# Nine expert-weight buffers and an fp32r scatter in a mixture-of-experts stage

## The reference

```python
hn2 = rms_norm(x, g_norm2) * (1.0 + scale2) + shift2
g_prob = softmax(hn2 @ w_rg + b_rg)                 # 4 groups, the best one is taken
e_top, e_loc = top_k(e_logits_of_that_group, 2)     # 2 of its 8 experts
e_w = softmax(e_top) * g_w
ffn[token] = sum over its 2 experts e of e_w * ((silu(h @ w_gate[e]) * (h @ w_up[e])) @ w_down[e])
x = x + gate2 * ffn
return rms_norm(x, g_final)
```

## Time and profile before

| | us |
|---|---|
| median of 3 runs | 1523.45 (1521.31 to 1524.22) |
| the profiled execution | 1520.18 |
| its span, first to last instruction | 1518.3 |
| PE busy | 1396.9 (92%) |
| DVE busy | 697.5 (46%) |
| ACT busy | 577.2 (38%) |
| POOL busy | 69.7 (5%) |
| DMA, mean over the span | 245 GB/s |

### The profile page before, as it was taken

The page is one execution under the profiler, slowest core; times in us unless marked ns, Lnnn a source line. Parts: engine busy times, 40 slices in busy tenths (PEclk is TensorE's granted clock), DMA queues, the critical chain, the costliest instruction groups (busy, mean ns, idle before and its releaser), DMA issues.

```text
span 1518.3 us, 20243 instructions
## 1 busy us (share of the span) xinstructions
PE 1396.9 (92%) x7966; PEld 1004.9 (66%) x7966; DVE 697.5 (46%) x1208; ACT 577.2 (38%) x869; POOL 69.7 (5%) x75
## 2 busy tenths in 40 slices
PE   6999889999899967899997998879999999999995
PEld 6988578888679845899985985554444444444442
DVE  4744556666455445677755655552112112112113
ACT  4343645555544394565554543321111111111111
POOL 1000000101000033100000002000000000000000
PEclk9999999999999977999998996789999999999998
DMA  8547237899443601265644453055999999999991
GB/s 312 203 169 274 84 111 240 299 315 355 174 167 141 247 1 56 78 199 179 222 169 150 158 175 111 0 221 224 415 429 428 429 429 429 429 428 428 428 429 77
DMA packets 105634, 372.48 MB, mean 245 GB/s; under 512 B 4189, under 2 KB 51581, under 8 KB 93169
## 3 DMA queue, kind: packets, MB, share of 16 engines
q1 hardware_dynamic: 97680, 344.07, 58.6%
q0 software_dynamic: 7904, 27.76, 5.3%
HBM read 370.75 MB, written 1.05 MB: 245 GB/s over the span
## 4 chain that ended last, share of the span: by engine, by line
PE 68%; DMA 17%; DVE 7%; ACT 3%; issue 2%; POOL 1%; SPq 0%; DVEq 0%; ACTq 0%; POOLq 0%
DMA ring<-in_w_expert_up_dram 16%; PE ps L522 14%; PE ps L1211 10%; PE ps L488 8%; PE ps L489 7%; PE ps L490 7%; PE ps L501 3%; PE ps L503 3%; PE ps L502 3%; PE ps L1232 2%; DVE w_low L425 2%; PE ps L1186 2%; PE ps L899 2%; PE ps L1194 1%; DMA ring<-in_ret_w_in_dram 1%
## 5 line engine op out<-in xcount | busy, mean ns | idle before, releaser
L425 DVE TENSOR_TENSOR w_low<-ring,w_high 128x1024 fp32r<-128x1024 f32 x260 | 307.8, 1225 | 244.1 <-ACT w_high L417 236.5
L417 ACT ACTIVATE w_high<-ring 128x1024 fp32r<-128x1024 f32 x264 | 264.8, 1052 | 232.8 <-PE ps L522 109.4
L488 PE MATMUL ps<-h_high,w_high 128*128 128x256 f32 x1088 | 312.7, 287 | 4.5 <-DVE w_low L425 2.6
L489 PE MATMUL ps<-h_low,w_high 128*128 128x256 f32 x1088 | 308.9, 284 | 0.0
L490 PE MATMUL ps<-h_high,w_low 128*128 128x256 f32 x1088 | 308.7, 284 | 0.0
L1211 PE MATMUL ps<-ring,arena 128*64 128x512 f32 x1024 | 224.9, 593 | 8.1 <-DMA ring<-in_w_expert_up_dram 6.3
L488 PEld LDWEIGHTS ps<-h_high,w_high 128*128 128x128 f32 x1088 | 209.8, 193 | 24.3 <-issue 18.9
L489 PEld LDWEIGHTS ps<-h_low,w_high 128*128 128x128 f32 x1088 | 209.9, 193 | 0.0
L490 PEld LDWEIGHTS ps<-h_high,w_low 128*128 128x128 f32 x1088 | 209.7, 193 | 0.0
L1211 PEld LDWEIGHTS ps<-ring,arena 128*64 128x64 f32 x1024 | 77.4, 137 | 152.4 <-issue 152.4
L2036 DVE TENSOR_TENSOR arena<-arena,ps 128x512 f32<-128x512 f32 x16 | 16.7, 1046 | 219.3 <-PE ps L1211 219.3
(11 more groups left out here) (327 smaller groups left out, 1506.0 us busy)
## 6 DMA issues: line engine op xcount, KB each, us to landing
ring<-in_w_expert_down_dram SPq DMA_DIRECT2D x32, 2048.0 KB, 12.3
ring<-in_w_expert_gate_dram SPq DMA_DIRECT2D x32, 2048.0 KB, 14.9
ring<-in_w_expert_up_dram SPq DMA_DIRECT2D x32, 2048.0 KB, 17.2
ring<-in_ffn_w_up_dram SPq DMA_DIRECT2D x44, 1024.0 KB, 7.7
ring<-in_ret_w_in_dram SPq DMA_DIRECT2D x11, 2048.0 KB, 8.2
ring<-in_ffn_w_down_dram SPq DMA_DIRECT2D x10, 2048.0 KB, 9.5
ring<-in_w_in_dram SPq DMA_DIRECT2D x7, 2048.0 KB, 8.1
gates<-in_w_ada_dram POOLq DMA_DIRECT2D x12, 1024.0 KB, 5.7
```

Source lines behind the costliest of these rows:

```text
L417: nc.scalar.activation(hi, raw, ACT.Copy).then_inc(hi_done, 1)
L425: last = eng.tensor_tensor(lo, raw, hi.bitcast(F32), ALU.subtract)
L488: nc.tensor.matmul(o, hi, hTh[:, k, :], start=(k == 0), stop=False)
L489: nc.tensor.matmul(o, hi, hTl[:, k, :], start=False, stop=False)
```

## The change

Buffers. `const` keeps only the tables that are used late; decay, cosine and sine go to the end of the arena (a second DMA at the start). The arena grows by them, and three new slots, 6 to 8, lie in its last 12288 columns. Their order of use is `HOMES`; tile N (two gates, two ups, two downs per pair) goes to `HOMES[N % 9]` when tile N - 9 has been used. Slots 6 to 8 wait for `l_t`. The last two down tiles come in halves. The router's four small loads move on POOL from the start of the mixer to behind `l_t`, since their place in the arena is used until then.

Arithmetic. PSUM banks 0 to 3 start with x (products with the identity). The weight of a token goes into the hidden layer (`wslot`, the maximum over a row of the turned selection), the selection for the scatter becomes 0/1, the down result is multiplied by gate2 and split in `y_hi` and `y_lo` (fp32r), and the scatter is eight fp32r products. The last norm reads PSUM, tile by tile.

Order. The loop runs over three pairs per trip. The scatter of pair j comes after the gate products of pair j + 1. The gather's first half comes before the turn of the hidden layer, its second behind it. After the last pair no further gather is done. The flag is loaded before the last pair's end instead of behind it.

```diff
+        HOMES = (2, 6, 7, 8, 0, 1, 3, 4, 5)
+        NS = len(HOMES)
+        TILES = 3 * NE
...
+        def landed(N):
+
+            s = HOMES[N % NS]
+            return ring_in[s], last_fill[s] + 16 * (N // NS + 1)
+
+        def used(N):
+
+            p, c = N // 6, N % 6
+            return (m_gu, 2 * p + 1 + c // 2, 2) if c < 4 else (m_dn, p + 1, 1)
...
+            def expert_load(N, i=None):
+                s, value, step = used(N - NS)
+                sp.wait_ge(s, value if i is None else i * (3 * step) + value)
+                dst, src, done = expert_tile(N, i)
+                sp.dma_start(dst[:, :, :], src).then_inc(done, 16)
...
+            for N in range(NS):
+                home = HOMES[N]
+                if home < 3:
+                    sp.wait_ge(*freed[holder[home]])
+                elif home < 6:
+                    sp.wait_ge(wide_mm, n_halves)
+                else:
+                    sp.wait_ge(l_t, 2)
+                dst, src, done = expert_tile(N)
+                sp.dma_start(dst[:, :, :], src).then_inc(done, 16)
...
+            pool.wait_ge(l_t, 2)
             pool.dma_start(wr[:, :, 0:NG], A["w_router_group_2"][0].rearrange("(p k) n -> p k n", p=P)).then_inc(r_in, 16)
...
-            clear_sums(2)
+            for t in range(NT):
+                for half in range(2):
+                    nc.tensor.matmul(ps[:, 2 * t + half, :], ident, x[:, t, half * C:(half + 1) * C], start=True,
+                                     stop=False, skip_group_check=True)
```

On TensorE the scatter and the loop:

```diff
+            def scatter(j, i=None):
+
+                pe.wait_ge(m_swt, at(j + 1, i, 3))
+                pe.wait_ge(m_ya, at(2 * j + 2, i, 6))
+                pe.wait_ge(m_yv, at(2 * j + 2, i, 6))
+                for t in range(NT):
+                    for y in (y_hi, y_lo):
+                        for half in range(2):
+                            last = nc.tensor.matmul(ps[:, 2 * t + half, :], selT[:, t * P:(t + 1) * P],
+                                                    y[:, half * C:(half + 1) * C], start=False, stop=False,
+                                                    skip_group_check=True)
+                    if t == 0 and i is None:
+                        last.then_inc(m_fin, 1)
+                last.then_inc(m_fin if i is None else m_sct, 1)
...
-                gather((PAIRS + 2) * r + 1, None)
-                with pe.Fori(0, PAIRS) as i:
...
-                    scatter(False)
-                    pe.wait_ge(m_h, i + (PAIRS * r + 1))
...
-                    gather(i + ((PAIRS + 2) * r + 2), i + (PAIRS * r + 1))
...
-                scatter(True)
+                first = PAIRS * r
+                for half in range(2):
+                    gather(first, half)
+                gate_or_up(first, 0)
+                turn_select(first)
+                with pe.Fori(0, PAIRS // 3) as i:
+                    for j in range(first, first + 3):
+                        gate_or_up(j, 1, i)
+                        gather(j + 1, 0, i)
+                        turn_hidden(j, i)
+                        gather(j + 1, 1, i)
+                        pe.wait_ge(m_hc, at(j + 1, i, 3))
+                        homes = [enter_tile(6 * j + 4 + e, i) for e in range(2)]
+                        down(homes, range(KE)).then_inc(m_dn, 1)
+                        gate_or_up(j + 1, 0, i)
+                        turn_select(j + 1, i)
+                        scatter(j, i)
+                j = first + PAIRS - 1
+                gate_or_up(j, 1)
+                turn_hidden(j)
+                pe.wait_ge(m_hc, j + 1)
+                for e in range(2):
+                    pe.wait_ge(half_in[e], 16 * (r + 1))
+                homes = [HOMES[(6 * j + 4 + e) % NS] for e in range(2)]
+                down(homes, (0, 1))
+                for e in range(2):
+                    enter_tile(6 * j + 4 + e)
+                down(homes, (2, 3)).then_inc(m_dn, 1)
+                scatter(j)
```

On ScalarE and VectorE:

```diff
+            def silu(j, i=None):
+                act.wait_ge(m_gu, at(2 * j + 1, i, 6))
+                if j % PAIRS:
+                    act.wait_ge(m_sct, at((PAIRS - 1) * (j // PAIRS) + j % PAIRS, i, 3))
+                nc.scalar.activation(hs, ps[:, 4, :], ACT.Silu).then_inc(m_si, 1)
...
+            nc.scalar.activation(credit[:, 7:8], const[:, 0:1], ACT.Sqrt)
+            expert_end(0)
...
-            norm_act(act, 7)
+                    expert_end(r)
+                act.wait_ge(m_fin, NT * PASSES)
+            for t in range(NT):
+                act.wait_ge(m_fin, t + 1)
+                nc.scalar.activation(xn[:, t, :].rearrange("p (h n) -> p h n", h=2), ps[:, 2 * t:2 * t + 2, :], ACT.Square,
+                                     accum_out=stat[:, 20 + t:21 + t]).then_inc(f_ss, 1)
+                act.wait_ge(f_ms, t + 1)
+                nc.scalar.activation(stat[:, 24 + t:25 + t], stat[:, 22 + t:23 + t], ACT.Sqrt).then_inc(f_sd, 1)
...
+            def turned(j, i=None):
+
+                dve.wait_ge(m_tr, at(j + 1, i, 3))
+                if j % PAIRS:
+                    dve.wait_ge(m_sct, at((PAIRS - 1) * (j // PAIRS) + j % PAIRS, i, 3))
+                nc.vector.tensor_reduce(wslot, ps[:, 6, 0:T], AX, ALU.max)
+                nc.vector.tensor_scalar(selT[:, :], ps[:, 6, 0:T], 0.0, None, ALU.is_gt).then_inc(m_swt, 1)
...
+            def gated(j, i=None):
+                dve.wait_ge(m_dn, at(j + 1, i, 3))
+                for half in range(2):
+                    cols = slice(half * C, (half + 1) * C)
+                    nc.vector.tensor_tensor(ye[:, cols], ps[:, 6 + half, :], gates[:, 1, cols], ALU.mult).then_inc(m_y, 1)
+                for half in range(2):
+                    cols = slice(half * C, (half + 1) * C)
+                    dve.wait_ge(m_ya, at(2 * j + 1 + half, i, 6))
+                    nc.vector.tensor_tensor(y_lo[:, cols], ye[:, cols], y_hi[:, cols].bitcast(F32), ALU.subtract)\
+                        .then_inc(m_yv, 1)
```

More of the change, by code:

```diff
@@ L526, in project, with gated_residual @@
                 last.then_inc(wide_mm, 1)
[L528 removed]
+        def gated_residual(link, g, bank, tmp, tiles):
             for t in tiles:
@@ L1176, in _ @@
             nc.tensor.matmul(ps[:, 5, 128:128 + NE], ones, asg[:, 1, :], start=False, stop=True).then_inc(t_lg, 1)
-            def gather(value, hgt):
-                pe.wait_ge(m_s, value)
-                for half in (1, 0):
-                    if half == 0 and hgt is not None:
-                        pe.wait_ge(m_hc, hgt)
-                    for k in range(4 * half, 4 * half + 4):
-                        for t in range(NT):
-                            last = nc.tensor.matmul(ps[:, 4 + half, (k % 4) * P:(k % 4 + 1) * P],
-                                                    xn[:, t, k * P:(k + 1) * P], sel[:, t, :],
-                                                    start=(t == 0), stop=(t == NT - 1))
-                    last.then_inc(m_ga, 1)
@@ new lines, in at, with gather @@
+            def at(value, i, step):
+                return value if i is None else i * step + value
+            def gather(j, half, i=None):
+                if half == 0:
+                    pe.wait_ge(m_s, at((PAIRS + 1) * (j // PAIRS) + j % PAIRS + 1, i, 3))
+                if j:
+                    pe.wait_ge(m_h if half else m_si, at(j, i, 3))
+                for k in range(4 * half, 4 * half + 4):
+                    for t in range(NT):
+                        last = nc.tensor.matmul(ps[:, 4 + half, (k % 4) * P:(k % 4 + 1) * P],
+                                                xn[:, t, k * P:(k + 1) * P], sel[:, t, :],
+                                                start=(t == 0), stop=(t == NT - 1))
+                last.then_inc(m_ga, 1)
@@ new lines, in enter_tile, with gate_or_up @@
+            def enter_tile(N, i=None):
+                s, value = landed(N)
+                pe.wait_ge(s, at(value, i, 32))
+                return HOMES[N % NS]
+            def gate_or_up(j, g, i=None):
+                if g == 0:
+                    pe.wait_ge(m_xa, at(j + 1, i, 3))
+                    pe.wait_ge(m_xv, at(j + 1, i, 3))
+                homes = [enter_tile(6 * j + 2 * g + e, i) for e in range(2)]
+                for k in range(KD):
+                    for e in range(2):
+                        last = nc.tensor.matmul(ps[e * R:(e + 1) * R, 4 + g, :], xg[:, k, e * R:(e + 1) * R],
+                                                wide[homes[e]][:, k, :], start=(k == 0), stop=(k == KD - 1))
+                last.then_inc(m_gu, 1)
@@ new lines, in down @@
+            def down(homes, ks):
+                for half in range(2):
+                    for k in ks:
+                        for e in range(2):
+                            last = nc.tensor.matmul(ps[e * R:(e + 1) * R, 6 + half, :], hgT[:, k, e * R:(e + 1) * R],
+                                                    tall[homes[e]][:, k, half * C:(half + 1) * C],
```

(35 more changed lines are left out.)

367 lines of the change are left out of this document (176 added, 191 removed).

## The result

The changed kernel takes 1495.5 us (median of 4 runs, 1494.17 to 1496.84); the kernel before, on the same chip, 1522.38 us. The ratio is 0.9823, with a 95% interval of 0.9806 to 0.984: faster by 1.8%. The forecast was 1495.4 us. Two later groups of runs on other occasions gave 1496.0 and 1496.54, beside 1523.17 and 1523.7 for the kernel before. The profiled run took 1494.17 us, 26.0 less than the profiled run of before; the working had foreseen 28.0. So the forecast's agreement with the median hides terms that were off by up to 1.8 us, and the rest of this document looks for them.

What follows compares the result with a forecast made beforehand. The stream of expert tiles was taken to bound the stage, narrowly ahead of TensorE. Gains of 17.0, 5.3 and 5.8 us, less 0.1 for the start, made 28.0 off 1523.45: 1495.4 us, range 1489 to 1506.

Steps and rivals of the forecast that it cites:

- Nine slots: Expert stage: three more tiles fetched before the first pair, so 87 instead of 90 remain after it; 14.7 us saved.
- The second hole: Stream loss at 1060 to 1080 us (387 of 429 GB/s), because down tiles' buffers come free late; 2.0 us saved.
- The price of a tile: Expert stream from 1042.0 us: one tile takes 4.894 us, from 90 tiles moved until 1484.5.
- TensorE per pair: Expert stage: a pair takes TensorE 27.4 us instead of 28.56, with scatter 1.97 and stall 0.35, against 29.4 of stream.
- Upper bound ... 28.9, which still hides: If fp32r scatter costs as much as fp32, a pair takes TensorE 28.9 us, still hidden under 29.4 of stream.
- TensorE binds: Rival: unseen hand-overs add 3 us a pair, so a pair takes 30.3 us and the kernel 1507; chance 0.10.
- The last pair: From the last up tile's landing to the last down's end: 16.8 us instead of 22.1, gain 5.3 us.
- The rival of the falling clock: Expert stage: at 1.2 GHz TensorE needs 54 us a pair; three pairs of sixteen give 1570 us; chance 0.04.
- The tail: From the last down's end to the kernel's end: 13.4 us instead of 19.2, gain 5.8 us.
- The rival of late tables: Router's four table DMAs, moved beside the tile stream, delay the router from 1010.38: +8.6 us, 1504; chance 0.09.
- The start: Kernel start: constants come in two DMAs instead of one, costing zero to 0.4 us; 0.1 taken off the gain.
- The signs: Wrong if data ends after 1470, router starts later, a mid-stage pair takes other than 29.4 us, or clock leaves 1.00.

Runs made afterwards that it cites:

- the upper group's with the later wait: Changed kernel with VectorE's wait for the constants put behind the third weight tile's split; its slower runs, 1503.31, 1503.85 and 1507.28 us, at first; 6 of 11 near 1504.

## Why the prediction held, and where its steps did not

*Nine slots, 14.7 us.* Right: 14.8 by six against nine slots. *The second hole, 2.0 us.* Right: 2.0, and by the order: it stayed closed with six slots, and with the fp32 scatter. *The price of a tile.* (1468.7 - 1042.4) / 87 = 4.90 us against 4.894, with 1042.4 from the 223 GB/s of 1040 to 1045.

*TensorE per pair.* 27.3 to 27.5 us against 27.4: right, but two terms were off against each other. The scatter takes 1.85 us, not 1.97, and the stall for the hidden copy was almost nothing, 0.03 to 0.05 in the chain, not 0.35, while the other steps came out that much longer.

*"Upper bound ... 28.9, which still hides", and "nothing of this reaches the end time".* This step is wrong, though it did no harm at 27.4. I compared periods, 28.9 with 29.4, and should have compared ends. TensorE's sum is 1041.0 (first up) + 15 x 27.4 = 1452.0; the stream's is 1460.8. The margin is 8.8 us in fifteen pairs, 0.6 us a pair. The fp32 scatter of 29.0 us a pair ended at 1478.7. So the slots and the cheap scatter are worth their 15 to 16 us only together, and the rival "TensorE binds", which I let begin with 3 us more a pair, begins with 0.6. For the same reason TensorE does not wait "for DMA before both gate and up" in the whole stage but only from 1333 us on.

*The last pair, 5.3 us.* The path was right (16.8 us in the run with six slots), its size here was not: 18.5 us, since the down product ran partly at the lower clock and took 8.81 instead of 7.04. The text had kept the clock high for the whole of the stage because it was 1.00 in the earlier trace rows; between the pairs it was, with idle times of at most 1.2 us (1.5 in the run with half the scatter). Behind the last up, TensorE is idle for 1.24 us, does four short turns and is idle for 0.69 us, and the clock is at 0.50 from about 1471 to 1474 us. With TensorE kept busy the down took 7.1 us in three of three profiles. The gaps alone do not say where the fall comes: of the ten profiles with the same two gaps, seven have it in the down, and three (six slots, the fp32 scatter, the upper group's with the later wait) kept 1.00 through the down and fell in the last scatter, as two of the three filled ones did. Of all the profiles here only that with 10 and 5 filling matmuls shows neither. So that the gaps bring the fall is likely and not shown, and so is what decides its place. The rival of the falling clock was thus right in its kind and wrong in its place and size: not 54 us a pair in mid-stage but 1 to 2 us, once. The Trainium skill, "TensorE: Matmul & The Clock Gate", section "A second HAM failure mode: psum-queue depth-cycling", tells of another kernel in which frequent micro-idles between groups of matmuls make the clock oscillate. In mid-stage, with two idles a pair from 1333 us on, the trace does not agree (1.00 from 1040 to 1470); at the end it has a single fall behind two gaps, which is no oscillation.

*The tail, 5.8 us.* Right at 6.1. The load of functions that it had counted at 1.28 us was there, and it was avoidable. The Trainium skill, "ScalarE: Activation LUTs", section "Table sets: the hidden batching unit", says that cheap functions such as relu and copy are in every set and that calls should be grouped by set. The run with the root asked for first agrees with the grouping, with one load in place of two; for the square, which the section does not place, it shows that it shares a set with the root.

*The router's tables.* The rival of late tables is out: their four loads took 8.0 to 12.3 us to land from about 975 us on, behind the first tiles, where the earlier trace rows has 3.0 us for one; they were there by 990, and the router's products started at 1011.33, 0.95 behind the earlier trace rows like all around them.

*The start, 0.1 us.* The profile gives 0.95 us at the router against the profile of before. It cannot be pinned on the change: three profiles of the unedited changed kernel have the first gate at 1033.52, 1035.09 and 1034.97, and of before there is one, of its fastest run. What the traces do show is a new gap of 3.50 us near 26 us, 0.74 in the kernel before, and a clock of 0.66 in the five microseconds after 30; the kernel before had its own loss earlier, where the same products take 0.41 us each up to 19.1 us and 0.28 behind it, after a gap of 1.24. The lower clock moved rather than came.

*The signs.* Three of the four signs of being wrong that the prediction names did show: the router started later (0.95 us), a pair in mid-stage took 27.4 us and not 29.4 up to 1306 us, and the clock left 1.00 in the last down. Only the end of the data, at 1468.7, stayed under its 1470. The second of them is the step above on ends and periods; none was large enough here to move the time out of the range.

That the median was met to 0.1 us is therefore partly luck: the terms of 16.8, 3.5 and 6.1 miss the predicted ones by +0.1, -1.8 and +0.3, the start by -0.7, while the base of the forecast, 1523.45 us, became 1522.38 with one more run, and the profiled run of before lay 2.2 us under that.

## What to carry to other kernels

When an engine's work runs beside a stream, compare the two ends and not the two periods: the stream has a lead as large as its buffers, so every further buffer shortens the period that the engine must keep to (here 28.0 us with nine buffers, against 29.4 of stream). Each extra buffer filled before the stage starts is worth one transfer, but only while that margin lasts.

Behind the last transfer every step is serial and TensorE is idle between steps: the products that are left may run at the lower clock, and work whose result is not used, sized to the gap, may hold it up (the down product was whole in three of three profiles with it, in three of ten without). A dummy call that chooses ScalarE's functions belongs behind the last branch.

## What the runs showed of the hardware

Transfers of sixteen-kilobyte rows held 427 to 430 GB/s for 400 us, also while TensorE was busy for 99.9 of 100 us. The eight passes of an fp32r scatter with 512 columns took 1.85 us against 3.44 for fp32. A matmul of 128x128 in fp32 with its own weights cost 0.24 us when nothing overlapped it. The granted clock stayed at 1.00 through idle times of up to 1.5 us between long products. Behind two gaps of 1.24 and 0.69 it fell to 0.50 for about 3 us in seven of ten profiles; in the other three, with the same gaps, it fell up to 10 us later.
